# One-hot matrices of the gate stage in token pairs: unit steps for VectorE, a step of two elements for TensorE

## Chip, cores and metric

The kernel runs on one core of one Trainium2 chip. The metric is the device time of one execution in microseconds (us), the median of several runs.

## What is computed

One layer on 256 tokens of width 1024: a mixer of sparse attention and a gated recurrence, a cross attention to 256 memory tokens, and a layer of product-key experts, each followed by a residual and a layer norm. The change lies in the expert layer. Of its reference:

```python
s1, i1 = lax.top_k(s[:, :, 0], PEER_TOPK)      # 16 of 128 keys, per token and head
s2, i2 = lax.top_k(s[:, :, 1], PEER_TOPK)
cand_s = (s1[..., :, None] + s2[..., None, :])  # 256 sums, 16 kept
top_s, top_pos = lax.top_k(cand_s, PEER_TOPK)
expert = jnp.take_along_axis(cand_i, top_pos, axis=-1)   # i1 * 128 + i2
gate = jax.nn.softmax(top_s, axis=-1)
a = jax.nn.gelu(jnp.einsum('ted,td->te', down[eb], tb), approximate=False)
out = jnp.einsum('te,ted->td', a * gb, up[eb])
```

There are 128 x 128 = 16384 experts, and each token takes 8 heads x 16 = 128 of them, each with a gate.

## The kernel before

It is written by hand for each engine, with semaphores between them. Weights are streamed from HBM in tiles of 128 x 1024 float32 (512 KB each), 331 of them: 75 for the projections of the first part, then 128 of the table `down`, then 128 of the table `up`. The kernel gathers no experts. It multiplies all tokens with all experts and weighs the result with a matrix of gates that is zero where a token did not choose an expert.

Every tile goes the same way. SyncE's queue fetches it into a ring of five buffers (`raw`, line 470), ScalarE rounds it to a short form (`hi`, four buffers, line 536), VectorE takes the rest `raw - hi` (`lo`, line 694, written over `raw`), and TensorE makes three matmuls where one would do, high by high, high by low and low by high. 44 tiles around the start of the tables get their `lo` from GpSimd instead (line 522).

- **down**: tile `j` holds 128 experts. TensorE forms their product with all 256 tokens in `psG`, 8 blocks of the width times three matmuls of 256 columns (lines 1088 to 1090). ScalarE writes gelu of it to `H[:, j, :]` (line 660), so that `H` is (partition = second key) x (tile = first key) x (token).
- **up**: tile `j` again holds 128 experts, now on the contracted side. `H[:, j, :]`, by then weighed with the gates, is split into `act_hi` (ScalarE, line 678) and `act_lo` (VectorE, line 1066), and TensorE makes 12 matmuls of 512 columns into `psS` and `psT` (line 1348).

**The gates** come between. For eight tokens (`TOK`) and one half of the first keys (`HALF` = 64) at a time, which gives 2 x 32 = 64 groups, VectorE runs `one_hot(g)`, four operations in float16 on all 128 partitions. A partition there is one of the 128 choices (head and rank) of a token:

- line 1032, `one2`: (8 tokens x 128 keys), 1 where the key is the choice's second key `i2T`
- line 1034, `same1`: (8 x 64), 1 where the key is its first key `i1T`
- lines 1037 and 1038, `one1_hi` and `one1_lo`: `same1` times the high and the low part of the gate

In each the token's value is an operand that stands still over the innermost dimension (its step there is 0), while `iota` and `same1` are read with a step of 1. TensorE's `gates(g)` then makes two matmuls for each of the eight tokens (lines 1332 and 1333), with `one2[k]` (128 x 128) as the weights and `one1_hi[k]` or `one1_lo[k]` (128 x 64) as the moving operand. So a group has 16 pairs of a weight load and a matmul of 64 columns. At last VectorE's `apply_gates(g)` (line 1047) multiplies the result in `psO` into `H`.

The order is a written list, `TABLE_ORDER`, which every engine walks:

```python
        while g < GROUPS and j >= HALF + g * 3 // 2:
            out.append(("gates", g))
...
        while g < 2 * GROUPS and j >= (g - GROUPS) * 39 // 20:
            out.append(("gates", g))
```

Groups 0 to 31 follow the tiles 64 to 110 of `down`, two groups to three tiles. Groups 32 to 63 follow the tiles 0 to 60 of `up`, about one group to two tiles. At "gates g" VectorE runs `one_hot(g + 1)` and then `apply_gates(g)`; `one2`, `one1_hi`, `one1_lo` and the halves of `psO` have two buffers each, `same1` has one. At every tile VectorE also makes the `lo` of the tile three places on, and in `up` the `act_lo` four places on. `apply_gates(g)` waits until TensorE has run `gates(g)`; `gates(g)` waits for `one_hot(g)`.

Of the kernel before, what the change touches and what calls it, by code (L numbers as in the profile page):

```python
# [7 lines left out]
F16 = mybir.dt.float16  # L8
# [3 lines left out]
ALU = mybir.AluOpType  # L12
AX = mybir.AxisListType

P = 128
# [14 lines left out]
NK = 128  # L30
# [41 lines left out]
HALF = E_TILES // 2  # L72
TOK = 8
# [173 lines left out]
def build(nc, a):  # L247
    from contextlib import ExitStack
    ctx = ExitStack()
    with ctx:  # L250
# [3 lines left out]
        def sb(name, shape, dt=FP32, at=None):  # L254
            size = int(np.prod(shape[1:])) * {FP32: 4, F32R: 4, BF16: 2, F16: 2, U32: 4}[dt]
            size = -(-size // 32) * 32
            where = place["at"] if at is None else at
            if at is None:
                place["at"] += size
            return nc.alloc_sbuf_tensor_at(name, shape, dt, offset=where)  # L260
# [4 lines left out]
        def sem(name):  # L265
            return ctx.enter_context(nc.semaphore(name))
# [39 lines left out]
        i1T = sb("i1T", [P, S], F16)  # L306
        i2T = sb("i2T", [P, S], F16)
        gT = sb("gT", [P, S])
        g_lo = sb("g_lo", [P, S], F16)
        g_hi = sb("g_hi", [P, S], F16)  # L310
# [2 lines left out]
        warm = sb("warm", [P, 8])  # L313
        route_at = place["at"]
        place["at"] += 288
        iota = sb("iota", [P, NK], F16)
        one2 = [sb(f"one2_{i}", [P, TOK, NK], F16) for i in range(2)]
        same1 = sb("same1", [P, TOK, HALF], F16)
        one1_hi = [sb(f"one1_hi{i}", [P, TOK, HALF], F16) for i in range(2)]
        one1_lo = [sb(f"one1_lo{i}", [P, TOK, HALF], F16) for i in range(2)]  # L320
        act_at = place["at"]
        place["at"] += 1024
        assert place["at"] <= nc.sbuf_usable_end, place["at"] - nc.sbuf_usable_end
# [9 lines left out]
        for i in range(RING, EARLY):  # L333
# [109 lines left out]
        one_ready, gates_done, gated = (  # L443
            sem("one_ready"), sem("gates_done"), sem("gated"))
# [241 lines left out]
        def _(dve):  # L686
            step = Steps(dve, dve_step)
# [127 lines left out]
            for i in range(2):  # L815
                half = slice(i * KD // 2, (i + 1) * KD // 2)
# [48 lines left out]
            for what, i in ORDER:  # L865
# [62 lines left out]
                elif what == "level" and i[0] < 8:  # L928
                    j, t = i
# [9 lines left out]
                    if t == 1 and j >= 1:  # L939

                        L = 1 << (j - 1)
                        n = HH * S // (2 * L)
# [29 lines left out]
                elif what == "turn":  # L972
                    t = i % 2
# [7 lines left out]
                elif what == "norm":  # L981
                    w, t = i
# [41 lines left out]
            def one_hot(g):  # L1024
                half, t0, s = g // GROUPS, g % GROUPS * TOK, g % 2
                if g >= 2:
                    dve.wait_ge(gates_done, g - 1)
                if g >= 1:
                    dve.wait_ge(one_ready, g)
                t = slice(t0, t0 + TOK)  # L1030
                mine = [P, TOK, HALF]
                dve.tensor_tensor(one2[s][:], iota[:].unsqueeze(1).broadcast_to([P, TOK, NK]),  # L1032
                                  i2T[:, t].unsqueeze(2).broadcast_to([P, TOK, NK]), ALU.is_equal)
                step(dve.tensor_tensor(same1[:], iota[:, half * HALF:(half + 1) * HALF].unsqueeze(1).broadcast_to(mine),  # L1034
                                       i1T[:, t].unsqueeze(2).broadcast_to(mine), ALU.is_equal))
                step.wait()
                dve.tensor_tensor(one1_hi[s][:], same1[:], g_hi[:, t].unsqueeze(2).broadcast_to(mine), ALU.mult)  # L1037
                dve.tensor_tensor(one1_lo[s][:], same1[:], g_lo[:, t].unsqueeze(2).broadcast_to(mine), ALU.mult)\  # L1038
                    .then_inc(one_ready, 1)

            def apply_gates(g):
                half, t0, s = g // GROUPS, g % GROUPS * TOK, g % 2
# [42 lines left out]
        def _(pe):  # L1085
# [136 lines left out]
            for what, i in ORDER:  # L1222
                if what == "gemm":
                    gemm(i)
                elif what == "hidden":
                    pe.wait_ge(blocks_ready, 1)
                    for kv in range(2):
                        for m in range(CB // 2):
                            mm = pe.matmul(psM[:, kv * G * NC:(kv + 1) * G * NC], w1[:, kv, m, :], blk[:, kv, m, :],
                                           start=m == 0, stop=m == CB // 2 - 1)  # L1230
                    mm.then_inc(hidden_done, 1)
                elif what == "compressed":
# [4 lines left out]
                    for g in range(G):  # L1237
                        mm = pe.matmul(psM[0:NC, 256 + g * HD:256 + (g + 1) * HD],
                                       hz[:, (G + g) * NC:(G + g + 1) * NC], w2[:, 1, :], start=True, stop=True)
# [7 lines left out]
                elif what == "level":  # L1247
                    j, t = i
# [7 lines left out]
                    for h in range(HH):  # L1256
                        if j == 8:
                            mm = pe.matmul(psM[:, h * P:(h + 1) * P], KB[:, h, 0:P], QF[:, h, P:S],
                                           start=True, stop=True)
                        else:  # L1260
                            mm = pe.matmul(psM[:, h * P:(h + 1) * P], KB[:, h, t * P:(t + 1) * P],  # L1261
                                           (hq if j == 0 else QF)[:, h, t * P:(t + 1) * P], start=True, stop=True)
                    mm.then_inc(level_done, 1)
                elif what == "read_out":
# [3 lines left out]
                    for h in range(HH):  # L1268
                        out = psO[:, i * 512 + h * P:i * 512 + (h + 1) * P]
                        mm = pe.matmul(out, att[:, h, i, :], hv[:, i, h * P:(h + 1) * P], start=True, stop=i == 0)  # L1270
                        if i == 1:
                            mm = pe.matmul(out, att_off[:, h, :], hv[:, 0, h * P:(h + 1) * P], start=False, stop=True)
                    mm.then_inc(read_done, 1)
                elif what == "route":
# [4 lines left out]
                    for u in range(i * NT, (i + 1) * NT):  # L1279
                        if u >= 4:  # L1280
                            pe.wait_ge(score_out, u - 3)
                        t = u % NT
# [3 lines left out]
                elif what == "turn":  # L1286
                    t = i % 2
# [14 lines left out]
                    for k in range(KD):  # L1302
# [4 lines left out]
                        mm = pe.transpose((psS, psT)[t][:, k * P:(k + 1) * P], src, ident[:])  # L1307
# [15 lines left out]
            def gates(g):  # L1323
                s = g % 2
                pe.wait_ge(one_ready, g + 1)
                if g == 0:
                    pe.wait_ge(index_out, 4)
                if g >= 2:
                    pe.wait_ge(gated, g - 1)
                out = psO[:, s * 512:(s + 1) * 512].rearrange("p (k j) -> p k j", k=TOK)  # L1330
                for k in range(TOK):
                    pe.matmul(out[:, k, :], one2[s][:, k, :], one1_hi[s][:, k, :], start=True, stop=False)  # L1332
                    mm = pe.matmul(out[:, k, :], one2[s][:, k, :], one1_lo[s][:, k, :], start=False, stop=True)
                mm.then_inc(gates_done, 1)

            def up(j):
# [17 lines left out]
            for what, j in TABLE_ORDER:  # L1354
# [6 lines left out]
                elif what == "index":  # L1361
                    pe.wait_ge(gate_ready, 1)
                    pe.wait_ge(score_out, PH * NT)
                    for q in range(3):
                        for t in range(NT):
                            src = (chosen[:, 0], chosen[:, 1], chosen_s[:])[q]
                            mm = pe.transpose(psO[:, q * S + t * P:q * S + (t + 1) * P],
                                              src[:, t * PH:(t + 1) * PH, :].rearrange("p h k -> p (h k)"), ident[:])
# [26 lines left out]
def constants():  # L1395
    bf = np.dtype("bfloat16")
    i = np.arange(P)
    s, t = i[:, None], i[None, :]
    masks = np.zeros((P, 8, P), np.float32)
    masks[:, 0] = s == t  # L1400
    for j in range(1, 8):
        masks[:, j] = (((s ^ t) >> (j - 1)) == 1) & (t > s)
    tok = (np.arange(NT)[None, :] * P + i[:, None])
    valid = (np.arange(NC) * CS + CB - 1)[None, None, :] <= tok[:, :, None]
    return {"ident": np.eye(P, dtype=np.float32), "identb": np.eye(P).astype(bf),
            "iota": np.broadcast_to(i[None, :], (P, NK)).astype(np.float16),
            "iota16": np.broadcast_to(np.arange(TOPK), (P, TOPK)).astype(np.float16),
            "causal": np.where(t > s, -1e30, 0.0).astype(bf),
            "cmp_mask": np.where(valid, 0.0, -1e30).astype(np.float32),
            "cmp_any": valid.any(-1).astype(np.float32),  # L1410
            "level_mask": masks.astype(bf)}
# [37 lines left out]
```

## Time and profile before

| | |
|---|---|
| median of 3 runs | 1200.07 us (1198.83 to 1202.44) |
| the profiled execution: its own time | 1201.39 us |
| its span | 1199.6 us |
| mean granted TensorE clock in it | 0.971 |
| TensorE matmul busy | 1106.3 us (92%) |
| TensorE weight loads | 994.0 us (83%) |
| VectorE | 842.6 us (70%) |
| ScalarE | 512.1 us (43%) |
| GpSimd | 145.2 us (12%) |
| DMA | 186.59 MB, mean 156 GB/s |

The span is the profiled stretch from the first instruction to the last; the execution's own time is 1.8 us longer, and 1.3 us above the median. Matmuls are pipelined: the row of one gives its whole length, and the next starts long before it ends, so a matmul's price in a stream is the distance from start to start, not its own duration. VectorE's rows overlap by some 0.08 us in the same way. Shares of busy time are averages over stages that have different limits.

### The profile page before, as it was taken

To read this page: it belongs to the slowest core of one execution; us is meant where nothing else is said; L and a number is where in the kernel's file an instruction comes from. 1 tells how busy PE (TensorE), PEld (TensorE's weight loads), DVE (VectorE), ACT (ScalarE), POOL (GpSimd) and SP (SyncE) were. 2 spreads that over 40 slices of the span, in tenths; PEclk is the share of its full clock that TensorE was granted. 3 is DMA by queue.
4 is the path that set the end of the run, shared out by engine and by line. 5 is a ranking of instruction groups with operands and counts; after the bars stand their busy time and mean duration, and the time that the engine had idled before them with its cause. 6 is when DMAs were issued, how large, how long until landed. Compare 5 with 4: busy or idle time off the path is not lost.

```text
span 1199.6 us, 19066 instructions
## 1 busy us (share of the span) xinstructions
PE 1106.3 (92%) x7790; PEld 994.0 (83%) x7790; DVE 842.6 (70%) x1363; ACT 512.1 (43%) x799; POOL 145.2 (12%) x77
## 2 busy tenths in 40 slices
PE   6999899998977988999999999999999899999995
PEld 6998789787767988999999888987777777888884
DVE  4435656673569996154799999559999998555555
ACT  4344423444334443554433334444444344554452
POOL 2000200000024899700000000000000000000000
PEclk9889979999989999999999999999999899999998
DMA  9732212463312654555544444565454455555562
GB/s 330 261 118 89 88 54 88 140 223 112 101 41 90 188 162 141 177 178 188 175 144 143 149 149 153 171 204 172 157 164 158 131 172 174 192 193 191 191 192 75
DMA packets 50440, 186.59 MB, mean 156 GB/s; under 512 B 5825, under 2 KB 5857, under 8 KB 49841
## 3 DMA queue, kind: packets, MB, share of 16 engines
q1 hardware_dynamic: 48384, 176.71, 45.3%
q0 software_dynamic: 1968, 8.66, 2.1%
q8 instruction: 62, 1.02, 0.4%
q14 instruction: 26, 0.20, 0.1%
HBM read 183.77 MB, written 1.05 MB: 154 GB/s over the span
## 4 chain that ended last, share of the span: by engine, by line
PE 56%; DVE 33%; issue 3%; POOL 3%; ACT 2%; DMA 2%; SPq 0%; DVEq 0%; ACTq 0%
DVE lo L694 11%; PE psG L1088 10%; PE psG L1089 10%; PE psG L1090 10%; PE psS L1348 8%; PE psT L1348 8%; DVE one L1032 6%; DVE one_hi L1037 3%; DVE same L1034 3%; DVE one_lo L1038 3%; POOL lo L522 3%; DVE act_lo L1066 2%; PE psS L1169 2%; DMA raw<-in_down 1%; PE psO L1261 1%
## 5 line engine op out<-in xcount | busy, mean ns | idle before, releaser
L536 ACT ACTIVATE hi<-raw 128x1024 fp32r<-128x1024 f32 x331 | 350.2, 1058 | 333.2 <-DMA raw<-in_up 175.7
L694 DVE TENSOR_TENSOR lo<-raw,hi 128x1024 fp32r<-128x1024 f32 x287 | 348.2, 1220 | 186.8 <-ACT hi L536 186.5
L1088 PE MATMUL psG<-b_hi,hi 128*128 128x256 f32 x1152 | 334.9, 291 | 9.3 <-POOL lo L522 7.8
L1089 PE MATMUL psG<-b_lo,hi 128*128 128x256 f32 x1152 | 329.0, 286 | 0.0
L1090 PE MATMUL psG<-b_hi,lo 128*128 128x256 f32 x1152 | 328.5, 285 | 0.0
L1088 PEld LDWEIGHTS psG<-b_hi,hi 128*128 128x128 f32 x1152 | 224.1, 195 | 11.3 <-POOL lo L522 9.0
L1089 PEld LDWEIGHTS psG<-b_lo,hi 128*128 128x128 f32 x1152 | 224.2, 195 | 0.2
L1090 PEld LDWEIGHTS psG<-b_hi,lo 128*128 128x128 f32 x1152 | 224.0, 194 | 0.0
L522 POOL TENSOR_TENSOR lo<-raw,hi 128x1024 fp32r<-128x1024 f32 x44 | 123.2, 2818 | 125.2 <-ACT hi L536 125.0
L660 ACT ACTIVATE H<-psG 128x256 f32<-128x256 f32 x128 | 49.1, 383 | 166.5 <-PE psG L1090 166.4
L1066 DVE TENSOR_TENSOR act_lo<-H,act_hi 128x256 fp32r<-128x256 f32 x128 | 53.8, 422 | 78.7 <-ACT act_hi L678 78.7
L1348 PE MATMUL psS<-hi,act_hi 128*128 128x512 f32 x256 | 82.6, 404 | 0.0
L1348 PE MATMUL psT<-hi,act_hi 128*128 128x512 f32 x256 | 79.9, 393 | 0.0
L1348 PE MATMUL psS<-lo,act_hi 128*128 128x512 f32 x256 | 79.9, 393 | 0.0
L1348 PE MATMUL psS<-hi,act_lo 128*128 128x512 f32 x256 | 79.8, 393 | 0.0
L1348 PE MATMUL psT<-lo,act_hi 128*128 128x512 f32 x256 | 79.7, 393 | 0.0
L1348 PE MATMUL psT<-hi,act_lo 128*128 128x512 f32 x256 | 79.4, 392 | 0.0
L1032 DVE TENSOR_TENSOR one<-iota,i2T 128x1024 f16<-128x1024 f16 x64 | 78.0, 1219 | 0.0
L1088 PE MATMUL psG<-o_hi,hi 128*128 128x256 f32 x192 | 58.5, 305 | 13.8 <-DVE lo L694 11.0
L1332 PEld LDWEIGHTS psO<-one_hi,one 128*128 128x128 f16 x512 | 31.9, 98 | 40.6 <-DVE one_lo L1038 37.5
L1332 PE MATMUL psO<-one_hi,one 128*128 128x64 f16 x512 | 39.5, 195 | 24.7 <-DVE one_lo L1038 24.7
L1089 PE MATMUL psG<-o_lo,hi 128*128 128x256 f32 x192 | 57.4, 299 | 0.0
(273 smaller groups left out, 1605.2 us busy)
## 6 DMA issues: line engine op xcount, KB each, us to landing
raw<-in_down SPq DMA_DIRECT2D x128, 512.0 KB, 3.8
raw<-in_up SPq DMA_DIRECT2D x128, 512.0 KB, 4.0
raw<-in_w_stream SPq DMA_DIRECT2D x75, 512.0 KB, 3.8
w<-in_w POOLq DMA_DIRECT2D x1, 2048.0 KB, 10.0
xT<-in_xT SPq DMA_DIRECT2D x2, 512.0 KB, 4.8
memT<-in_memT SPq DMA_DIRECT2D x1, 1024.0 KB, 7.9
x_tok<-in_x_tok POOLq DMA_DIRECT2D x1, 1024.0 KB, 5.1
ln_gb<-in_ln_g POOLq DMA_DIRECT2D x2, 512.0 KB, 6.4
```

The source lines that it names most:

```text
L522: pool.tensor_tensor(lo[slot(n)][:], raw[slot(n)][:], hi[n % DEPTH][:].bitcast(FP32), ALU.subtract)\
L536: act.activation(hi[n % DEPTH][:], raw[slot(n)][:], ACT.Copy).then_inc(hi_done, 1)
L660: act.activation(H[:, j, :], psG[j % 2][:, 0:S], ACT.Gelu).then_inc(h_out, 1)
L694: dve.tensor_tensor(lo[slot(n)][:], raw[slot(n)][:], hi[n % DEPTH][:].bitcast(FP32), ALU.subtract)\
L1032: dve.tensor_tensor(one2[s][:], iota[:].unsqueeze(1).broadcast_to([P, TOK, NK]), i2T[:, t].unsqueeze(2).broadcast_to([P, TOK, NK]), ALU.is ...
L1034: step(dve.tensor_tensor(same1[:], iota[:, half * HALF:(half + 1) * HALF].unsqueeze(1).broadcast_to(mine), i1T[:, t].unsqueeze(2).broadcas ...
L1066: dve.tensor_tensor(a_lo[j % 4][:], H[:, j, :], a_hi[j % 4][:].bitcast(FP32), ALU.subtract)\
L1088: pe.matmul(out, hi_l, hi_r, start=start, stop=False)
L1089: pe.matmul(out, hi_l, lo_r, start=False, stop=False)
L1090: return pe.matmul(out, lo_l, hi_r, start=False, stop=stop)
L1332: pe.matmul(out[:, k, :], one2[s][:, k, :], one1_hi[s][:, k, :], start=True, stop=False)
L1348: mm = pe.matmul((psS, psT)[t][:, c * 512:(c + 1) * 512], left[:, cut], right[:, c * 512:(c + 1) * 512], start=st, stop=sp)
```

## The change

The four float16 operands keep their size but are laid out in pairs of tokens. `one2` was (token, key) and becomes (pair of tokens, key, token of the pair); `same1`, `one1_hi` and `one1_lo` likewise. `iota` holds each number twice. The token's value is now read as (pair, standing still over the keys, token of the pair), so that its innermost dimension has two elements with a step of 1, as has every other operand of the four operations. The counts of elements, the instructions, their order and every wait stay as they are. TensorE's weights and moving operands are the columns of one token, which now lie two elements (4 bytes) apart.

```diff
-        iota = sb("iota", [P, NK], F16)
-        one2 = [sb(f"one2_{i}", [P, TOK, NK], F16) for i in range(2)]
-        same1 = sb("same1", [P, TOK, HALF], F16)
-        one1_hi = [sb(f"one1_hi{i}", [P, TOK, HALF], F16) for i in range(2)]
-        one1_lo = [sb(f"one1_lo{i}", [P, TOK, HALF], F16) for i in range(2)]
+        iota = sb("iota", [P, NK, 2], F16)
+        one2 = [sb(f"one2_{i}", [P, TOK // 2, NK, 2], F16) for i in range(2)]
+        same1 = sb("same1", [P, TOK // 2, HALF, 2], F16)
+        one1_hi = [sb(f"one1_hi{i}", [P, TOK // 2, HALF, 2], F16) for i in range(2)]
+        one1_lo = [sb(f"one1_lo{i}", [P, TOK // 2, HALF, 2], F16) for i in range(2)]
...
-                t = slice(t0, t0 + TOK)
-                mine = [P, TOK, HALF]
-                dve.tensor_tensor(one2[s][:], iota[:].unsqueeze(1).broadcast_to([P, TOK, NK]),
-                                  i2T[:, t].unsqueeze(2).broadcast_to([P, TOK, NK]), ALU.is_equal)
-                step(dve.tensor_tensor(same1[:], iota[:, half * HALF:(half + 1) * HALF].unsqueeze(1).broadcast_to(mine),
-                                       i1T[:, t].unsqueeze(2).broadcast_to(mine), ALU.is_equal))
+
+                def pairs(x, n):
+                    return x[:, t0:t0 + TOK].rearrange("p (k b) -> p k b", b=2).unsqueeze(2)\
+                        .broadcast_to([P, TOK // 2, n, 2])
+
+                def columns(c0, n):
+                    return iota[:, c0:c0 + n, :].unsqueeze(1).broadcast_to([P, TOK // 2, n, 2])
+                dve.tensor_tensor(one2[s][:], columns(0, NK), pairs(i2T, NK), ALU.is_equal)
+                step(dve.tensor_tensor(same1[:], columns(half * HALF, HALF), pairs(i1T, HALF), ALU.is_equal))
                 step.wait()
-                dve.tensor_tensor(one1_hi[s][:], same1[:], g_hi[:, t].unsqueeze(2).broadcast_to(mine), ALU.mult)
-                dve.tensor_tensor(one1_lo[s][:], same1[:], g_lo[:, t].unsqueeze(2).broadcast_to(mine), ALU.mult)\
-                    .then_inc(one_ready, 1)
+                dve.tensor_tensor(one1_hi[s][:], same1[:], pairs(g_hi, HALF), ALU.mult)
+                dve.tensor_tensor(one1_lo[s][:], same1[:], pairs(g_lo, HALF), ALU.mult).then_inc(one_ready, 1)
...
-                    pe.matmul(out[:, k, :], one2[s][:, k, :], one1_hi[s][:, k, :], start=True, stop=False)
-                    mm = pe.matmul(out[:, k, :], one2[s][:, k, :], one1_lo[s][:, k, :], start=False, stop=True)
+                    pe.matmul(out[:, k, :], one2[s][:, k // 2, :, k % 2], one1_hi[s][:, k // 2, :, k % 2], start=True, stop=False)
+                    mm = pe.matmul(out[:, k, :], one2[s][:, k // 2, :, k % 2], one1_lo[s][:, k // 2, :, k % 2], start=False, stop=True)
...
-            "iota": np.broadcast_to(i[None, :], (P, NK)).astype(np.float16),
+            "iota": np.broadcast_to(i[None, :, None], (P, NK, 2)).astype(np.float16),
```

## Rows read from the trace of the kernel before

**Rows 1.** Busy time by stretch (length; PE, PEld, DVE, ACT, POOL), granted clock, DMA share, GB/s

```profile
584.00:749.00 165.00, 152.66 (x1620) 148.92 (x1619) 163.92 (x202) 65.39 (x94) 0.00 (x0) 1.00 0.46 148
749.00:798.00 49.00, 49.00 (x410) 49.00 (x410) 25.16 (x25) 23.48 (x34) 0.00 (x0) 1.00 0.54 181
798.00:1003.00 205.00, 192.62 (x1248) 152.07 (x1247) 201.29 (x277) 84.68 (x125) 1.09 (x2) 0.98 0.51 163
```

**Rows 2.** The chain that ended last, from 584 to 749 us, by line

```profile
by line: DVE lo L694 33.2%; DVE one L1032 21.3%; DVE one_hi L1037 12.6%; DVE same L1034 11.5%; DVE one_lo L1038 11.4%; issue 7.0%; DVE H L1047 3.3%; PE psO L1332 0.2%; PE psO L1333 0.1%
```

**Rows 3.** VectorE in order of time, one group within the down table (start, duration)

```profile
605.63 1.22 DVE L1032 TENSOR_TENSOR one<-iota,i2T 128x1024 f16<-128x1024 f16 x1
606.76 0.68 DVE L1034 TENSOR_TENSOR same<-iota,i1T 128x512 f16<-128x512 f16 x1
607.48 0.69 DVE L1037 TENSOR_TENSOR one_hi<-same,g_hi 128x512 f16<-128x512 f16 x1
...
608.69 0.68 DVE L1047 TENSOR_TENSOR H<-psO,H 128x512 f32<-128x512 f32 x1
609.29 1.22 DVE L694 TENSOR_TENSOR lo<-raw,hi 128x1024 fp32r<-128x1024 f32 x1
610.43 1.22 DVE L1032 TENSOR_TENSOR one<-iota,i2T 128x1024 f16<-128x1024 f16 x1
```

**Rows 4.** VectorE in the up table: the same step of two groups in turn

```profile
860.76 1.22 DVE L1032 TENSOR_TENSOR one<-iota,i2T 128x1024 f16<-128x1024 f16 x1
...
867.36 1.22 DVE L1032 TENSOR_TENSOR one<-iota,i2T 128x1024 f16<-128x1024 f16 x1
```

**Rows 5.** ScalarE's gelu of two down tiles, 18 tiles apart, before the gates begin

```profile
529.61 0.38 ACT L660 ACTIVATE H<-psG 128x256 f32<-128x256 f32 x1 [0.84 <-PE psG L1090]
...
581.45 0.38 ACT L660 ACTIVATE H<-psG 128x256 f32<-128x256 f32 x1 [0.25 <-PE psG L1090]
```

**Rows 6.** TensorE in order of time: group 0 from first matmul to the next tile, and group 31

```profile
584.13 0.20 PE L1332 MATMUL psO<-one_hi,one 128*128 128x64 f16 x1
...
584.60 0.36 PE L1088 MATMUL psG<-b_hi,hi 128*128 128x256 f32 x1
...
748.38 0.20 PE L1332 MATMUL psO<-one_hi,one 128*128 128x64 f16 x1 [0.83 <-DVE one_lo L1038]
```

**Rows 7.** TensorE: start of up, a long wait, groups without wait (three apart), end of gates

```profile
797.89 0.63 PE L1348 MATMUL psS<-hi,act_hi 128*128 128x512 f32 x2
...
936.64 0.23 PE L1332 MATMUL psO<-one_hi,one 128*128 128x64 f16 x1 [3.12 <-DVE one_lo L1038]
...
945.38 0.20 PE L1332 MATMUL psO<-one_hi,one 128*128 128x64 f16 x1
...
963.60 0.20 PE L1332 MATMUL psO<-one_hi,one 128*128 128x64 f16 x1
...
1002.32 0.71 PE L1348 MATMUL psS<-hi,act_hi 128*128 128x512 f32 x2
```

**Rows 8.** VectorE in float16 while GpSimd runs, in order of time

```profile
434.45 2.62 POOL L522 TENSOR_TENSOR lo<-raw,hi 128x1024 fp32r<-128x1024 f32 x1 [0.59 <-ACT hi L536]
434.85 10.77 DVE L1001 TENSOR_TENSOR picked_e<-iota,picked_f 128x8192 f16<-128x8192 f16 x1
437.12 10.70 POOL L522 TENSOR_TENSOR lo<-raw,hi 128x1024 fp32r<-128x1024 f32 x1
...
445.66 4.31 DVE L1008 TENSOR_TENSOR picked_e<-picked_e,ranked_f 128x4096 f16<-128x4096 f16 x1
...
460.94 3.44 POOL L522 TENSOR_TENSOR lo<-raw,hi 128x1024 fp32r<-128x1024 f32 x1
...
462.16 3.30 DVE L1013 TENSOR_TENSOR picked_e<-picked_e 128x1024 f16<-128x1024 f16 x1
```

**Rows 9.** TensorE: eight pairs with float32 weights and 64 columns, and what follows

```profile
78.01 1.00 PE L1216 MATMUL psO<-vg,probsT 128*128 128x64 f32 x8
78.82 0.36 PE L1088 MATMUL psG<-o_hi,hi 128*128 128x256 f32 x1
```

## The prediction

> **What bounds the kernel now.** I read the busy time by stretch first, then the chain of waits, then VectorE and TensorE in order of time. Averaged over the kernel TensorE looks like the limit, but the stretches that hold the 64 gate groups differ from their neighbours. From 584 to 749 us VectorE is busy for 163.92 of 165 us and TensorE has 12.3 us without work; from 798 to 1003 us it is 201.29 of 205 us, and TensorE lacks 12.4 us. In between, where no group lies, TensorE is busy for all 49 us and VectorE for half [rows 1]. The chain of the first stretch says the same: nearly all of it is VectorE, and its four one-hot operations alone make 56.8% (21.3 + 12.6 + 11.5 + 11.4) [rows 2]. So in these two stretches, and only there, VectorE sets the pace.
>
> How much could go is the distance between VectorE's pace and TensorE's. **VectorE's period**: from start to start the four one-hot operations take 1.13, 0.72 and twice 0.605 us (1.21 for the pair), applying the gates takes 0.60 and the `lo` of a tile 1.14 [rows 3]. A group is 605.63 to 609.29 = 3.66 us. In `down` two groups and three tiles make 2 x 3.66 + 3 x 1.14 = 10.74 us. In `up` a group and two tiles make 6.60 us [rows 4], which leaves (6.60 - 3.66 - 2.28) / 2 = 0.33 us for one `act_lo` of 256 elements.
>
> **TensorE's period**: 18 tiles of `down` without gates pass in 581.45 - 529.61 = 51.84 us, 2.88 us each [rows 5]. A group takes 584.60 - 584.13 = 0.47 us for its 16 pairs, 0.029 us a pair, and I add 0.09 us, since the first matmul behind it is 0.08 us longer than usual (0.36 against 0.28 us): 0.56 us [rows 6]. Two groups and three tiles are then 3 x 2.88 + 2 x 0.56 = 9.76 us, against VectorE's 10.74. In `up`, between 945.38 and 963.60 us, TensorE was behind after a wait and ran three periods without one: 6.07 us each, against VectorE's 6.60 [rows 7].
>
> **The change, part by part.**
>
> *VectorE.* No instruction is added, taken away or moved. 4 x 64 operations change their access patterns. Does that make them faster? The rows of the index step show it, if GpSimd is taken out. There VectorE and GpSimd take turns: an operation of one runs only once the other's has ended. The operation of 8192 elements with one operand at an innermost step of 0, as in the gates now, could start when GpSimd ended at 434.45 + 2.62 = 437.07 us and ended at 445.62: 8.55 us, 1.04 ns an element. The next, of 4096 elements, all three operands in float16 with an innermost step of 1 and one of them repeated over a middle dimension, could start at 437.12 + 10.70 = 447.82 and ended at 449.97: 2.15 us, 0.52 ns an element, half [rows 8]. That is the pattern that the change gives, except that its repeated rows are two elements long and not 16. At half the price per element, 1024 elements cost what 512 cost now, and 512 what 256 cost: `one2` 1.13 to 0.60, `same1` 0.72 to 0.45 (with its 0.12 of waiting for its own result), the other two 0.605 to 0.33 each. The group falls from 3.66 to 0.60 + 0.45 + 0.66 + 0.60 = 2.31 us. VectorE's periods become 2 x 2.31 + 3.42 = 8.04 us in `down` and 6.60 - 1.35 = 5.25 us in `up`, both below TensorE's 9.76 and 6.07. The margin is wide: a group of up to 3.1 us would still do ((9.76 - 3.42) / 2 = 3.17; 3.66 - 0.53 = 3.13), so about 0.5 of the 1.35 us is needed and the rest is idle time on VectorE, worth nothing.
>
> What rows of two elements cost has only a distant row. The last halving of the index step reads and writes rows of two float16, 32 bytes apart, in all three operands: it could start at 460.94 + 3.44 = 464.38 and ended at 465.46, 1.08 us for 1024 elements, twice the price [rows 8]. That is the upper bound, no gain at all; the lower bound is 0.52 ns an element. I take the lower. In the change only the token's value has short rows, it stays on one word of 4 bytes, and output and first operand run through memory without gaps. The 8192-element operation also stayed on one word, 16 times over, and paid nothing for that.
>
> The Trainium skill, "Vector Engine (DVE) Microarchitecture Reference", section "Measured stream behaviour on trn2", speaks against the change here: a port keeps its full rate only in runs of at least two neighbouring words of 4 bytes, and one source that hops for every word costs 1.73 instead of 1.05 ns. By an estimate from that page `one2` would take 0.95 us and a group 3.2 us, which puts VectorE and TensorE level and the time some 3 us above the forecast. The trace agrees for short rows that hop, by its 1.08 us; for a word that is read again it has only the operation with a step of 0, which paid nothing.
>
> *TensorE.* 1024 pairs (16 x 64) read weights and moving operand 4 bytes apart. Below: 0.029 us a pair, as now; the float32 matmuls of the tables also read a column every 4 bytes and lose nothing by it, at 256 columns in 0.12 us (2.88 / 24). Above: eight pairs of float32 weights with 64 columns took 78.82 - 78.01 = 0.81 us, 0.101 us each [rows 9]; they make more passes, so this is far above. I take 0.029 for the sum, because moving data at a 4-byte step is what all the big matmuls do; the weights are the open point and go into the rivals.
>
> *The rest.* The table `iota` doubles to 512 bytes a partition and is fetched once, before the gates begin, as one DMA of the same queue as before: 0. With VectorE ahead, `apply_gates(g)` will wait for TensorE's `gates(g)`. Behind it in VectorE's queue stand the next `act_lo` and `lo`, needed three tiles (8 us) later: 0. The DMA must deliver a tile per 2.9 us and did so at 181 GB/s where TensorE set the pace [rows 1]: 0.
>
> **The sum.** First stretch: from group 0 to group 31, 748.38 - 584.13 = 164.25 us. At TensorE's pace it is 46 tiles x 2.88 + 31 groups x 0.56 = 149.8 us: 14.4 us less. Second: 797.89 to 1002.32 = 204.43 us for 61 tiles and 32 groups. At 6.07 us per two tiles and a group, which is 2.755 a tile with 0.56 for the group, it is 168.1 + 17.9 = 186.0 us: 18.4 us less. The 3.12 us wait at 936.64 and what the clock lost in that stretch (0.98 granted) are in this difference [rows 1, 7]; an uninterrupted TensorE should not see them. Together 32.8 us. The profiled execution took 1201.4 us, so 1168.6; it lay 1.3 us above the median, so I forecast 1167 us.
>
> **The rivals.**
>
> *A. The forecast*: weights as fast as now, 1167 us, give or take 5 for group costs and the state of the rings.
>
> *B. The weight loads get somewhat slower.* For: float16 weights are packed two to a word of 4 bytes now, and each word would hold one useful element. At twice the price, 0.058 us a pair, 1024 x 0.029 = 29.7 us come back on TensorE, which nothing hides once it sets the pace: 1197 us. The Trainium skill, "TensorE: Matmul & The Clock Gate", section "Weight-path perf modes", has a fast weight load that reads weights 32 bits at a time, two of bf16, in chunks "packed or strided"; by the first half the rate would halve, by the second it is kept. No row here has 16-bit weights with a step.
>
> *C. The weight loads lose much*, as with a float32 load. This one ends slower. It decides from 0.029 + 32.8 / 1024 = 0.061 us a pair. At the upper bound of 0.101, TensorE pays 1024 x 0.072 = 73.7 us and the time is 1167 + 74 = 1241 us, with VectorE idle. For: rows 9 have the same 128 weights and 64 columns at 4 bytes an element. Against: those loads belong to float32 products.
>
> *D. The operations do not get faster*, because rows of two elements are no pattern for the faster rate, or the repeated word costs as much as it brings. Then VectorE still sets the pace and hides up to 0.5 us a group on TensorE: 1200 us. For: the 1.08 us in rows 8. Against: it takes the loss of more than half of the gain in every operation.
>
> **The chances.** A 0.60, B 0.17 (of which a tenth ends within 0.3% or above), C 0.13, D 0.10. 0.3% is 3.6 us, about what a measurement of this kernel can tell. Faster: A and most of B, 0.75. Same: D and a rest of B, 0.11. Slower: C and a little of B, 0.14. The range leaves out C and a thin tail below: 1159 to 1203 us. A alone would be 1162 to 1173.
>
> **What would show it.** Right: rows of `one` near 0.69 us instead of 1.22, of `same`, `one_hi`, `one_lo` near 0.42 instead of 0.68; in the gated stretches TensorE busy throughout, VectorE waiting for it at line 1047's new place, periods of 9.8 and 6.1 us, no granted clock below 1. B or C: `one` at 0.69 us, and the start-to-start distance of the 16 pairs above 0.029 us. D: `one` still near 1.2 us and periods of 10.7 and 6.6 us. Wrong in another way: TensorE waiting in these stretches for `lo`, `act_lo` or a DMA instead.

## The result and the profile after

| | before | after |
|---|---|---|
| median | 1201.26 us (4 runs, 1198.83 to 1205.91) | 1169.91 us (4 runs, 1168.0 to 1175.24) |
| profiled execution | 1201.39 us | 1171.79 us |
| TensorE matmul busy | 1106.3 us (92%) | 1101.7 us (94%) |
| VectorE busy | 842.6 us (70%) | 761.5 us (65%) |

The ratio is 0.9744, with a 95% interval of 0.9717 to 0.9771. The change saves 2.6% of the time. The forecast was 1167 us within 1159 to 1203.

Busy time of the kernel after, by stretch: groups 0 to 31, the tiles without gates, groups 32 to 63 (PE, PEld, DVE, ACT, POOL, then the granted clock, DMA share and GB/s):

```profile
587.00:737.00 150.00, 150.00 (x1605) 148.66 (x1602) 125.08 (x202) 64.52 (x92) 0.00 (x0) 1.00 0.50 162
737.00:786.00 49.00, 49.00 (x422) 49.00 (x421) 22.70 (x24) 25.02 (x36) 0.00 (x0) 1.00 0.55 180
786.00:973.00 187.00, 187.00 (x1250) 150.77 (x1250) 163.35 (x278) 83.91 (x124) 1.09 (x2) 1.00 0.55 179
```

TensorE is now busy throughout all three stretches, where it had lacked 12.3 and 12.4 us [rows 1]. VectorE, which had been full, idles for 25 and 24 us. The clock of the last stretch is 1.00 instead of 0.98. The chain that ended last, from 587 to 737 us, holds no VectorE line at all, where [rows 2] held little else:

```profile
by line: PE psG L1090 31.0%; PE psG L1091 29.4%; PE psG L1092 29.3%; PE psO L1334 5.3%; PE psO L1335 5.0%
```

VectorE in order of time, kernel after, one group within `down` (answers to rows 3; line 1037 is the old 1032):

```profile
606.21 0.68 DVE L1037 TENSOR_TENSOR one<-iota,i2T 128x1024 f16<-128x1024 f16 x1
606.81 0.42 DVE L1038 TENSOR_TENSOR same<-iota,i1T 128x512 f16<-128x512 f16 x1
607.27 0.43 DVE L1040 TENSOR_TENSOR one_hi<-same,g_hi 128x512 f16<-128x512 f16 x1
607.61 0.42 DVE L1041 TENSOR_TENSOR one_lo<-same,g_lo 128x512 f16<-128x512 f16 x1
607.95 0.68 DVE L1049 TENSOR_TENSOR H<-psO,H 128x512 f32<-128x512 f32 x1
608.55 1.22 DVE L694 TENSOR_TENSOR lo<-raw,hi 128x1024 fp32r<-128x1024 f32 x1
```

From start to start these are 0.60, 0.46, 0.34, 0.34 and 0.60 us, 2.34 us for the group in place of 3.66 [rows 3]. What VectorE waits for in these 386 us is ScalarE's `hi` and `act_hi` (kernel after, 587 to 973 us; total, times, longest):

```profile
DVE lo L694 <- ACT hi L536: 48.2, 30, 2.9
DVE act_lo L1068 <- ACT act_hi L678: 24.4, 29, 2.2
```

By stretch this is 23.9 us for `hi` in the first and 22.5 us for `act_hi` in the last; the rest lies between them, where no group is. No wait stands at line 1049, `apply_gates`: by the time VectorE comes to it, TensorE has made the group. The one applied at 607.95 us above ran on TensorE from 606.39 to 606.88 us.

TensorE in order of time, kernel after: group 0 and the tile behind it, group 31, the start of `up`, two groups in turn there, and the end of the gates (answers to rows 6 and 7):

```profile
586.85 0.20 PE L1334 MATMUL psO<-one_hi,one 128*128 128x64 f16 x1
586.88 0.20 PE L1335 MATMUL psO<-one_lo,one 128*128 128x64 f16 x1
...
587.34 0.36 PE L1090 MATMUL psG<-b_hi,hi 128*128 128x256 f32 x1
...
736.89 0.20 PE L1334 MATMUL psO<-one_hi,one 128*128 128x64 f16 x1
...
786.42 0.63 PE L1350 MATMUL psS<-hi,act_hi 128*128 128x512 f32 x2
...
853.27 0.20 PE L1334 MATMUL psO<-one_hi,one 128*128 128x64 f16 x1
...
859.32 0.20 PE L1334 MATMUL psO<-one_hi,one 128*128 128x64 f16 x1
...
972.72 0.71 PE L1350 MATMUL psS<-hi,act_hi 128*128 128x512 f32 x2
```

The first stretch, group 0 to group 31, takes 736.89 - 586.85 = 150.0 us instead of 164.25. The second takes 972.72 - 786.42 = 186.3 us instead of 204.43. A group's 16 pairs take 0.49 us, 0.0306 us each, against 0.47 and 0.029 in group 0 before [rows 6]; nearly all groups before took 0.47 or 0.48 us.

### The profile page after: what moved, and what is told of

Its sections match the earlier page's. It is cut to its first block, busy times and chain, and to the rows that moved or that the text cites. A ratio compares the mean times of both kernels' runs of the same rounds, so it can differ in the third digit from the quotient of the medians.

```text
span 1170.0 us, 19066 instructions
## 1 busy us (share of the span) xinstructions
PE 1101.7 (94%) x7790; PEld 996.2 (85%) x7790; DVE 761.5 (65%) x1363; ACT 512.9 (44%) x799; POOL 146.1 (12%) x77
## 3 DMA queue, kind: packets, MB, share of 16 engines
HBM read 183.80 MB, written 1.05 MB: 158 GB/s over the span
## 4 chain that ended last, share of the span: by engine, by line
PE 87%; DVE 5%; POOL 3%; ACT 2%; DMA 2%; issue 1%; SPq 0%; DVEq 0%; ACTq 0%
PE psS L1350 15%; PE psG L1090 15%; PE psT L1350 15%; PE psG L1091 14%; PE psG L1092 14%; POOL lo L522 3%; PE psS L1171 2%; PE psO L1334 1%; PE psO L1335 1%; PE psO L1263 1%; DMA raw<-in_down 1%; ACT hi L536 1%; PE psO L1231 1%; DVE lo L694 1%; PE psS L1163 1%
## 5 line engine op out<-in xcount | busy, mean ns | idle before, releaser
L1090 PEld LDWEIGHTS psG<-b_hi,hi 128*128 128x128 f32 x1152 | 224.4, 195 | 11.1 <-POOL lo L522 8.9
L1090 PE MATMUL psG<-o_hi,hi 128*128 128x256 f32 x192 | 59.2, 308 | 13.7 <-DVE lo L694 10.9
L1092 PE MATMUL psG<-o_hi,lo 128*128 128x256 f32 x192 | 57.9, 302 | 0.0
L1350 PEld LDWEIGHTS psT<-hi,act_hi 128*128 128x128 f32 x256 | 48.1, 188 | 10.7
L1350 PEld LDWEIGHTS psS<-lo,act_hi 128*128 128x128 f32 x256 | 48.1, 188 | 10.7
```

Source lines behind the costliest of these rows:

```text
L1090: pe.matmul(out, hi_l, hi_r, start=start, stop=False)
L1092: return pe.matmul(out, lo_l, hi_r, start=False, stop=stop)
L1350: mm = pe.matmul((psS, psT)[t][:, c * 512:(c + 1) * 512], left[:, cut], right[:, c * 512:(c + 1) * 512], start=st, stop=sp)
```

## Experiments

The theory: the operations of VectorE run at twice their rate, because all their operands are 16 bits wide with an innermost step of 1. A group needed to fall only to about 3.1 us for TensorE to take over, and the step of two elements costs TensorE next to nothing. Each part was tried by itself. Where an expectation speaks of a difference, its base is the kernel after. For runs with a single timed execution a ratio is not given.

### The step without the doubled rate

```diff
-        i1T = sb("i1T", [P, S], F16)
-        i2T = sb("i2T", [P, S], F16)
+        i1T = sb("i1T", [P, S])
+        i2T = sb("i2T", [P, S])
...
-        same1 = sb("same1", [P, TOK // 2, HALF, 2], F16)
+        same1 = sb("same1", [P, TOK // 2, HALF, 2])
```

> The paired layout with TensorE's step of two elements as in the change, but the two index tables and same1 are float32, so that each of the four one-hot operations has an operand that is not 16 bits wide. Theory (the gain is VectorE's doubled rate, the step costs TensorE nothing): the operations go back to 1.22 and 0.68 us, the periods to 10.7 and 6.6 us, the 16 pairs of a group stay 0.030 us apart, and the time is that of before, 1201 us. Rival (part of the gain comes from the layout itself, for instance from TensorE's reads or from the pair pattern alone): clearly below 1195 us with the operations shorter than 1.22 us. Rival (the step costs TensorE something that the change hides): above 1203 us, or pairs further apart.

1200.41 us against 1202.07 for the kernel before on the same chip, ratio 0.9984 (0.9964 to 1.0005): no difference. Groups of VectorE in this run, from 560 to 1000 us, and what TensorE waited for, from 560 to 1010 us:

```profile
L1037 DVE TENSOR_TENSOR one<-iota,i2T 128x1024 f16<-128x1024 f16 x62 | 75.5, 1218 | 0.0
L1038 DVE TENSOR_TENSOR same<-iota,i1T 128x512 f32<-128x512 f16 x62 | 42.4, 684 | 0.0
```

```profile
PE psO L1334 <- DVE one_lo L1041: 24.4, 39, 3.1
```

With one wide operand the operation takes 1218 ns again, and TensorE waits 24.4 us for the one-hots. So the layout by itself brings nothing; all of the gain is the rate. TensorE's part of the change was in this run too (0.49 us for 16 pairs, from 586.51 to 587.00 us), and while VectorE is the bound it costs nothing.

### How much of VectorE's saving was needed

In `one2_only`, `same1`, `one1_hi` and `one1_lo` keep the old layout and the old operations:

```diff
                 dve.tensor_tensor(one2[s][:], columns(0, NK), pairs(i2T, NK), ALU.is_equal)
-                step(dve.tensor_tensor(same1[:], columns(half * HALF, HALF), pairs(i1T, HALF), ALU.is_equal))
+                t = slice(t0, t0 + TOK)
+                mine = [P, TOK, HALF]
+                step(dve.tensor_tensor(same1[:], iota1[:, half * HALF:(half + 1) * HALF].unsqueeze(1).broadcast_to(mine),
+                                       i1T[:, t].unsqueeze(2).broadcast_to(mine), ALU.is_equal))
...
```

> Only one2 is in pairs; same1, one1_hi and one1_lo are as before. VectorE's group is 3.66 - 0.53 = 3.13 us, its periods 2 x 3.13 + 3.42 = 9.68 us in down and 6.07 us in up, level with TensorE's 9.77 and 6.05. Theory (of the 1.33 us taken from a group only about 0.5 was needed, then TensorE is the bound): 1170 to 1173 us, the whole gain from one operation of four. Rival (the gain follows VectorE's saved time, all of it counts): 0.53 / 1.33 of 31 us, so about 1189 us.

1171.54 us, ratio to before 0.9747 (0.9704 to 0.9790), where the whole change has 0.9744. The rival's 1189 us is out. Busy time in a piece of either gated stretch (same columns as above):

```profile
590.00:730.00 140.00, 140.00 (x1493) 138.71 (x1492) 138.27 (x187) 59.95 (x87) 0.00 (x0) 1.00 0.50 163
800.00:960.00 160.00, 158.45 (x1059) 127.69 (x1059) 159.10 (x238) 71.26 (x105) 0.00 (x0) 1.00 0.54 173
```

Both engines are full at once, 140.00 and 138.27 of 140 us: the two are level, as the periods of 9.68 and 9.77 us say. One operation of the four carries the whole gain, as far as these times can tell. The other way round, work was added to VectorE, operations like `one2` into a buffer that nobody reads:

```diff
+                dve.tensor_tensor(junk[:], columns(0, NK), pairs(i2T, NK), ALU.is_equal)
                 dve.tensor_tensor(one2[s][:], columns(0, NK), pairs(i2T, NK), ALU.is_equal)
                 step(dve.tensor_tensor(same1[:], columns(half * HALF, HALF), pairs(i1T, HALF), ALU.is_equal))
                 step.wait()
+                dve.tensor_tensor(junk[:], columns(0, NK), pairs(i2T, NK), ALU.is_equal)
```

The first `+` line alone is `one_more`, both are `two_more`.

> The change with one more operation like one2 in every group, into a buffer that nobody reads. VectorE's group grows by 0.60 to 2.92 us, its periods to 9.26 and 5.86 us, still under TensorE's 9.77 and 6.05. Theory (VectorE has idle time in both stretches): 1170 us, no change beyond 0.3%. Rival (VectorE still shares the bound): 64 x 0.60 = 38 us more at most, anything over 1175 us.

> The change with two more such operations in every group. VectorE's group is 3.52 us, its periods 10.46 and 6.46 us, above TensorE's 9.77 and 6.05. Theory (the bound moves back to VectorE at 3.1 us a group): 16 x 0.69 + 32 x 0.41 = 24 us more, 1194 us. Rival (VectorE's idle time is larger than the periods say, TensorE stays the bound): 1170 us. Rival (each added operation counts whole): 1170 + 77 = 1247 us.

One more: 1170.03 us, ratio 0.9708 (0.9673 to 0.9744). 64 x 0.60 = 38 us of work on VectorE cost nothing. Two more: 1191.29 us, ratio 0.9894 (0.9858 to 0.9931). The same two pieces, first of `one_more`, then of `two_more` with what TensorE waited for from 560 to 1010 us:

```profile
590.00:730.00 140.00, 139.81 (x1482) 138.45 (x1481) 132.67 (x216) 59.43 (x86) 0.00 (x0) 1.00 0.50 162
800.00:960.00 160.00, 160.00 (x1063) 128.94 (x1062) 157.28 (x268) 71.71 (x105) 0.00 (x0) 1.00 0.53 173
```

```profile
590.00:730.00 140.00, 132.95 (x1397) 129.75 (x1397) 139.12 (x227) 55.90 (x81) 0.00 (x0) 1.00 0.46 152
800.00:960.00 160.00, 153.13 (x1002) 121.21 (x999) 159.15 (x274) 67.50 (x99) 0.00 (x0) 1.00 0.50 165
```

```profile
PE psO L1337 <- DVE one_lo L1044: 17.7, 39, 3.0
```

The bound changes sides between a group of 2.92 and one of 3.52 us, and `one2_only` puts it at about 3.1. In the trace of `two_more` groups 0 and 31 lie 161.15 us apart, 11.1 more than after, where 11 was expected; the second stretch takes 199.14 us, 12.8 more, where 13 was expected. Its median is 21 and not 24 us above that of the kernel after; what could move such a median by 3 us stands in the last section: in this trace group 0 starts 5.2 us earlier than in that of the kernel after.

### Where a step begins to cost TensorE

The rivals B and C of the prediction asked whether the weights lose their rate when they lie 4 bytes apart. They don't, so wider steps were tried. With fours (`quads`) and eights (`octets`) the layout is the same with another number:

```diff
-        one2 = [sb(f"one2_{i}", [P, TOK // 2, NK, 2], F16) for i in range(2)]
+        one2 = [sb(f"one2_{i}", [P, TOK // 8, NK, 8], F16) for i in range(2)]
...
-                    pe.matmul(out[:, k, :], one2[s][:, k // 2, :, k % 2], one1_hi[s][:, k // 2, :, k % 2], start=True, stop=False)
+                    pe.matmul(out[:, k, :], one2[s][:, k // 8, :, k % 8], one1_hi[s][:, k // 8, :, k % 8], start=True, stop=False)
...
```

> Tokens laid out by fours: TensorE's operands have a step of four elements, 8 bytes, VectorE's innermost rows have four elements. Theory (neither step nor row length costs anything at this size): one2 0.68 us, pairs 0.030 us apart, 1170 us. Rival (a wider step slows the weight load or the moving operand): pairs further apart than 0.030 us, and 1024 times the difference more in time; at twice the distance 31 us more, 1200 us.

> All eight tokens of a group innermost: TensorE's operands have a step of eight elements, 16 bytes. The two theories of the run with fours, one doubling further. If the step costs TensorE nothing at all, 1170 us with pairs 0.030 us apart. If each read has a reach within which a step is free, 16 bytes is where I expect it to end: pairs 0.05 to 0.10 us apart, 1024 x 0.02 to 0.07 us more, 1190 to 1242 us, with VectorE's operations still at 0.68 and 0.42 us.

These ran once each: 1198.19 and 1260.12 us, beside 1201.76 for the kernel before. Each in turn, TensorE in order of time, from the first matmul of group 0 to the next tile:

```profile
582.65 0.23 PE L1334 MATMUL psO<-one_hi,one 128*128 128x64 f16 x1
...
583.62 0.36 PE L1090 MATMUL psG<-b_hi,hi 128*128 128x256 f32 x1
```

```profile
585.38 0.32 PE L1334 MATMUL psO<-one_hi,one 128*128 128x64 f16 x1
...
587.26 0.37 PE L1090 MATMUL psG<-b_hi,hi 128*128 128x256 f32 x1
```

At 8 bytes a pair takes 0.97 / 16 = 0.061 us, at 16 bytes 1.88 / 16 = 0.118 us. The theory expected fours to be free and was wrong; the rival's 1200 us is what came. VectorE's operations stayed at 685 and 419 ns in both, so row lengths of 2, 4 and 8 are all the same to them. Which operand it is was tried by giving eights to one of them alone (one line of each run's edit, the weights first):

```diff
+                    pe.matmul(out[:, k, :], one2[s][:, k // 8, :, k % 8], one1_hi[s][:, k // 2, :, k % 2], start=True, stop=False)
...
+                    pe.matmul(out[:, k, :], one2[s][:, k // 2, :, k % 2], one1_hi[s][:, k // 8, :, k % 8], start=True, stop=False)
...
```

> Only the weights (one2) have all eight tokens innermost, a step of 16 bytes; the moving operands stay in pairs. With both at 16 bytes a pair of load and matmul took 0.1175 us. Theory W (the load of the weights is what a wide step slows): pairs about 0.118 us apart, the weight load row still near 146 ns, 1258 us. Theory M (it is the moving operand): pairs 0.031 us apart, 1170 us. If both share it, something between.

> The reverse: the weights in pairs, the moving operands (one1_hi and one1_lo) with a step of 16 bytes. Theory W: pairs 0.031 us apart, 1170 us. Theory M: pairs up to 0.118 us apart, 1258 us. If a moving operand too is slowed by a step of 16 bytes, but less than the weights, since it has 64 columns and not 128, about 0.05 to 0.06 us and 1190 to 1200 us.

One execution each: 1202.82 us with the weights at 16 bytes, 1252.60 us with the moving operand, beside 1204.37 for before. The same rows, weights at 16 bytes first:

```profile
585.54 0.25 PE L1335 MATMUL psO<-one_hi,one 128*128 128x64 f16 x1
...
586.53 0.36 PE L1091 MATMUL psG<-b_hi,hi 128*128 128x256 f32 x1
```

```profile
584.97 0.28 PE L1335 MATMUL psO<-one_hi,one 128*128 128x64 f16 x1
...
586.75 0.37 PE L1091 MATMUL psG<-b_hi,hi 128*128 128x256 f32 x1
```

| bytes between elements: weights, moving | us a pair | time, us | 1170 + 1024 x (pair - 0.031) |
|---|---|---|---|
| 2, 2 (kernel before) | 0.029 | bound by VectorE | |
| 4, 4 (the change) | 0.031 | 1169.9 | 1170 |
| 8, 8 | 0.061 | 1198.2 | 1201 |
| 16, 16 | 0.118 | 1260.1 | 1259 |
| 16, 4 | 0.062 | 1202.8 | 1202 |
| 4, 16 | 0.111 | 1252.6 | 1252 |

Both operands are slowed, neither theory W nor M was right alone, and I had the order wrong: 64 moving columns at 16 bytes cost more than 128 weights. The two costs do not add up: 0.031 with 0.031 more for the weights and 0.080 more for the moving operand would be 0.142 us, and with both a pair takes 0.118, close to the 0.111 of the moving operand alone. The times are the median of four for the change and single executions below it. The last column says that what a pair gains in length reaches the end, to within 3 us, as it must once TensorE is the bound. The change sits on the last step that is free: one doubling more would have given back nearly all of it.

### Why the short rows of the index step were slow

```diff
-        iota = sb("iota", [P, NK, 2], F16)
+        iota = sb("iota", [P, NK, 8], F16)
...
-                    return iota[:, c0:c0 + n, :].unsqueeze(1).broadcast_to([P, TOK // 2, n, 2])
+                    return iota[:, c0:c0 + n, 0:2].unsqueeze(1).broadcast_to([P, TOK // 2, n, 2])
...
```

> The change, but iota holds each number's pair at a distance of 16 bytes, so that the first operand of one2 and same1 jumps from word to word; the rest is as in the change. It asks why the rows of two elements in the index step ran at the old rate (1.08 us for 1024 elements) while the change's rows of two run at the new one. Theory (jumping between words costs, reading one word again does not): one2 rises from 0.68 to between 0.95 and 1.22 us, same1 from 0.42 to between 0.56 and 0.68 us, one_hi and one_lo stay at 0.42, and the time stays at 1170 us, since a group of 2.8 to 3.1 us is still hidden. Rival (it was the length of the rows or of the output's rows): one2 stays at 0.68 us.

1171.62 us in its one execution. VectorE's groups, 560 to 1000 us:

```profile
L1037 DVE TENSOR_TENSOR one<-iota,i2T 128x1024 f16<-128x1024 f16 x63 | 68.0, 1079 | 0.0
L1038 DVE TENSOR_TENSOR same<-iota,i1T 128x512 f16<-128x512 f16 x63 | 38.6, 612 | 0.0
L1041 DVE TENSOR_TENSOR one_lo<-same,g_lo 128x512 f16<-128x512 f16 x63 | 26.4, 419 | 0.0
```

An operand that jumps from word to word costs 1079 - 685 = 394 ns for 512 words, 0.77 ns a word. The Trainium skill, "Vector Engine (DVE) Microarchitecture Reference", section "Measured stream behaviour on trn2", gives 1.73 against 1.05 ns for one source that hops 4 KiB at every element of 4 bytes, 0.68 more; the trace, with hops of 16 bytes, agrees in kind and comes out a little above. A word that is read again for every key costs nothing, which is why the paired token value works although its rows have two elements. The time did not move, since VectorE's group is still short enough to be hidden.

### The next limit: VectorE holds up GpSimd

In the index step TensorE waits for `lo` tiles of GpSimd, and GpSimd for VectorE's long operations (rows 8). Two versions were built on the change. In the first the operation of 8192 elements is cut in four:

```diff
+            n = 2 * PH * NT * TOPK // 4
+            for part in range(4):
+                some = slice(part * n, (part + 1) * n)
+                step(dve.tensor_tensor(picked_e[:].rearrange("p c n a -> p (c n) a")[:, some, :],
...
```

> The change with the 8192-element operation of the index step cut into four of 2048. It does not test the prediction but the next limit: GpSimd had to wait for that operation for some 8 us, and TensorE for GpSimd's lo for 4.5 us. Theory (GpSimd gets a turn between the parts, so the lo comes in time): that wait of 4.5 us goes, the time falls by 3 to 6 us to about 1166 us, and VectorE's index step grows by 6 us, which its 20 us of waiting for the exponentials hides. Rival (GpSimd is only late elsewhere, since its turns come every 4.4 us and TensorE needs a tile every 2.9): the wait moves to later tiles, less than 2 us gained.

1168.48 us, ratio 0.9715 (0.9676 to 0.9754), not to be told from the change. In its trace TensorE's waits for GpSimd fell only from 7.5 us (longest 4.5) to 6.6 us (longest 1.3, eight times). The rival was right: one long wait became eight short ones on later tiles. VectorE and GpSimd still take turns, one operation each, and the four parts together are no shorter than the whole. In the second the operation gets the pairs of the change:

```diff
-        ranked_f = sb("ranked_f", [P, PH * NT, 2, TOPK], F16)
-        picked_e = sb("picked_e", [P, 2, PH * NT * TOPK, TOPK], F16)
-        iota16 = sb("iota16", [P, TOPK], F16)
+        ranked_f = sb("ranked_f", [P, PH * NT, 2, TOPK, 2], F16)
+        picked_e = sb("picked_e", [P, 2, PH * NT * TOPK // 2, TOPK * 2], F16)
+        iota16 = sb("iota16", [P, TOPK, 2], F16)
...
+            n = PH * NT * TOPK
+            step(dve.tensor_tensor(picked_e[:].rearrange("p c n (a b) -> p (c n) a b", b=2),
+                                   iota16[:].unsqueeze(1).broadcast_to([P, n, TOPK, 2]),
+                                   picked_f[:].rearrange("p c (n b) -> p (c n) b", b=2).unsqueeze(2)
+                                   .broadcast_to([P, n, TOPK, 2]), ALU.is_equal))
...
-            for half in (8, 4, 2):
+            for half in (16, 8, 4):
```

> The change, with the same pairs in the index step too: picked_e is laid out in pairs of choices, iota16 and ranked_f hold each number twice, so the 8192-element operation has a step of 1 everywhere, and the rows of the halvings are twice as long. Theory (GpSimd is held up by the length of VectorE's operations): the 8.5 us of that operation become 4.3, the last halving (1.08 us, rows of two) becomes 0.6; TensorE's wait of 4.5 us for GpSimd's lo shrinks to about 1 us, and the time falls by 3 to 5 us to about 1166 us. Rival (GpSimd's turns, one per operation of VectorE, are what counts, as the run with four parts showed for its waits): under 2 us.

**1161.74 us** (1159.63 to 1164.82), ratio to before 0.9644 (0.9614 to 0.9673): better than both kernels, by 8 us over the change, where 3 to 5 were expected (the kernel before, timed beside each of the two, had 1204.37 and 1201.26 us; by the ratios to it the step is 12 us). This run, in order of time, and TensorE's waits for GpSimd from 380 to 590 us:

```profile
438.60 2.40 POOL L522 TENSOR_TENSOR lo<-raw,hi 128x1024 fp32r<-128x1024 f32 x1 [0.31 <-ACT hi L536]
438.61 6.68 DVE L1004 TENSOR_TENSOR picked_e<-iota,picked_f 128x8192 f16<-128x8192 f16 x1
```

```profile
PE psG L1093 <- POOL lo L522: 3.7, 4, 1.2
```

The operation could start at 441.00 and ended at 445.29 us: 4.29 us for 8192 elements where it had taken 8.55. The last halving, whose rows now have four elements, fell from 1.08 to 0.56 us: it could start when GpSimd ended at 460.64 + 3.38 = 464.02 us and ended at 464.58.

```profile
460.64 3.38 POOL L522 TENSOR_TENSOR lo<-raw,hi 128x1024 fp32r<-128x1024 f32 x1
461.80 2.78 DVE L1016 TENSOR_TENSOR picked_e<-picked_e 128x1024 f16<-128x1024 f16 x1
```

TensorE's waits went from 7.5 to 3.7 us, and the clock did more than I had expected. From 430 to 480 us, first the kernel after, then this run, then the run with four parts:

```profile
430.00:480.00 50.00, 42.37 (x330) 41.11 (x330) 41.16 (x26) 19.67 (x28) 49.11 (x14) 0.97 0.46 146
```

```profile
430.00:480.00 50.00, 46.34 (x380) 45.53 (x379) 37.11 (x20) 22.26 (x32) 48.60 (x17) 1.00 0.52 165
```

```profile
430.00:480.00 50.00, 43.60 (x351) 42.18 (x350) 48.87 (x31) 20.99 (x30) 48.58 (x14) 1.00 0.48 155
```

In the same 50 us TensorE gets through 380 matmuls instead of 330. 50 matmuls at 0.12 us are 6 us, of which 3.8 are waits and the rest goes with the clock. In both runs that lack the one long wait of 4.5 us the granted clock is 1.00; that the wait is what lowers it was not tried by itself. Not all of the 8 us need be the edit's: this trace reaches group 0 at 580.06 us, 6.8 earlier than after, and the last section shows that equal kernels differ there by several us.

## Why the prediction was right

**The bound.** VectorE in the two gated stretches and not between them: shown by the stretch between them (49 us in both kernels) and by `one_more` and `two_more`; the second moves the bound back. "Only there" says too much for the whole kernel: ahead of the tables TensorE waits once for a `lo` of VectorE, 11.0 us before and 10.9 after, and the change touches nothing of it.

**VectorE's part.** Forecast 0.69 and 0.42 us an operation and 2.31 us a group; measured 0.68, 0.42 and 2.34. The evidence had been in the index step, under GpSimd's turns: 2.15 us for 4096 elements with all steps of 1 against 8.55 us for 8192 with a step of 0 [rows 8]. The choice of the lower bound for rows of two was right for the reason given: `hop16` shows that jumping between words costs the rate where the length of the rows does not, and the last halving got its rate back with rows of two words. The estimate of 0.95 us for `one2`, by which a word that is read again counts as a jump, did not come: from start to start it takes 0.60 us.

**How much of it counts.** "About 0.5 of the 1.35 us is needed": `one2_only` saves 0.53 and has the whole gain.

**TensorE's pace.** 149.8 us forecast for the first stretch, 150.0 measured; 186.0 and 186.3 for the second. The periods are 9.77 and 6.05 us against 9.76 and 6.07. The sum of 32.8 us stands against 14.2 + 18.1 = 32.3 us. Taking a group at 0.56 us rather than the 0.47 that its pairs alone take was needed for this; measured it is (150.0 - 46 x 2.88) / 31 = 0.57 us.

**What VectorE waits for.** One sign did not come. `apply_gates` was to wait for TensorE's `gates`, and it never did: VectorE was held earlier in its list, at the `lo` or `act_lo`, by ScalarE. The prediction had put such a wait at 0 in the sum, and the wait that came cost nothing either, so the time is unmoved by it.

**The step of two elements.** Taken at no cost, 0.029 us a pair; measured 0.0306. Set beside the groups before, 0.47 or 0.48 us each, the 0.49 or 0.50 after are about 1 us over all 64. Rivals B and C did not come. A loss of their size exists one doubling further on, at 8 bytes, and at 16 bytes it hits the moving operand harder than the weights that I suspected. Row and argument for the moving operand (float32 columns 4 bytes apart) held at this step and not at 8 bytes, where a pair takes 0.061 us.

**From the sum to the median.** The profiled execution fell by 1201.39 - 1171.79 = 29.6 us, 2.7 less than the two stretches lost. All of that lies ahead of the gates: group 0 starts at 586.85 us after and at 584.13 before, in code that the change hardly touches. The median came out 2.9 us above the forecast of 1167.

## What to carry to other kernels

A one-hot by broadcast gets VectorE's doubled rate for 16-bit operands if a pair of neighbours is made the innermost dimension, so that even the broadcast operand has a step of 1 there; the pair costs only a table that is written twice. What the engine that reads the result pays for the step has to be priced too: here 4 bytes between elements were free for TensorE and 8 bytes doubled the time of a load and a matmul of 64 columns. And of a saving on the bounding engine only the part down to the next engine's pace counts, which can be read from two periods before anything is changed.

## What was not expected

- A pair of load and matmul is slowed by a step of 8 bytes already. With 64 columns it takes 0.031, 0.061 and 0.118 us at 4, 8 and 16 bytes, close to doubling each time. Whether weights or moving operand are behind the 0.061 was not tried; at 16 bytes each of them costs by itself.
- The stretch ahead of the gates, the same in all these kernels but the last two built on the change, differs between executions by some 5 us: group 0 starts between 581.62 us (`two_more`) and 586.85 us (after). The work and the waits are nearly the same, the granted clock is not. From 120 to 300 us, kernel after and then `two_more`:

```profile
120.00:180.00 60.00, 54.27 (x347) 47.79 (x347) 33.01 (x53) 20.58 (x46) 7.02 (x3) 0.89 0.21 70
240.00:300.00 60.00, 53.16 (x325) 47.87 (x324) 31.65 (x37) 26.11 (x42) 2.71 (x5) 0.95 0.54 177
```

```profile
120.00:180.00 60.00, 53.89 (x380) 47.96 (x379) 35.52 (x57) 21.65 (x48) 7.02 (x3) 0.97 0.25 80
240.00:300.00 60.00, 52.01 (x336) 46.79 (x334) 32.00 (x40) 27.30 (x49) 2.72 (x5) 1.00 0.48 162
```

  At 0.97 and 1.00 instead of 0.89 and 0.95, TensorE gets through 380 and 336 matmuls in the time of 347 and 325. That would explain the spread of a few us between medians of equal kernels; it was read off these profiles and not tested.
- VectorE's waits for `hi` and `act_hi` (47 us in the two gated stretches) look like a problem in the profile after, and `one_more` shows that they are none: 38 us of work were put in their place at no cost.
